# Seams between layers: x transposed before the whole last product, rounded tiles signalled one by one, half of a weight split moved behind the second rows

## The chip, the cores and the metric

The kernel runs on one core of a Trainium2 chip. TensorE (PE in the profile) multiplies and transposes, ScalarE (ACT) and VectorE (DVE) work on what it leaves in PSUM and on the weights, GpSimd (POOL) does small statistics and some loads, SyncE (SP) issues the loads of the weights. The metric is the time of one execution on the device in microseconds; of each kernel several executions are timed and the median is given. One further execution was taken with the hardware profiler, and all rows of the trace come from it.

## The reference

Two blocks of two layers each are applied to x, 256 rows of 1024 numbers. Each layer normalizes x, applies a mixer (attention with a state-space branch, a gated linear recurrence, and two kinds of attention with a memory) and adds the result; then it normalizes again, applies a gated feed-forward network and adds that result.

```python
# first block: the result is normalized before it is added
hn = rms_norm(x, norm_mix_pre[layer])
mix = even_mixer(hn, ...)  or  odd_mixer(hn, ...)
x = x + rms_norm(mix, norm_mix_post[layer])
hn = rms_norm(x, norm_ffn_pre[layer])
x = x + rms_norm(swiglu(hn, w_gate, w_up, w_down), norm_ffn_post[layer])

# second block: the result is added as it is
h = _rmsnorm(x, norm_mix[i])
x = x + jnp.concatenate([mix, mem_out], axis=-1) @ w_out[i]
x = x + _swiglu(_rmsnorm(x, norm_ffn[i]), w_gate_up[i], w_down[i])
```

So x is updated eight times, and seven of these updates are followed at once by a product of the new x with the next weights. These seven places are the seams. They are numbered 1 to 7 here, as `ed` is in the code (`ed` 0 is the first use of x, `ed` 8 the last update). At seams 1 to 4 the result is normalized before it is added, at seams 5 to 7 it is added as it is.

## The kernel before

**Products.** Every float32 product is made as three products of rounded values: each operand is held as a rounded high part and a rest (`WH` and `WL` for the weights, `HTh` and `HTl` for the transposed x, `YAh` and `YAl` for other inputs), and high by high, high by rest and rest by high are added in PSUM. Lines 452 to 454 are these three in most places; lines 487, 488 and 490 are the same three in `edge_product`, which is used for the first product after a seam.

**Weights.** They come in 200 chunks of 128 x 2048 numbers, in the order of use, through three buffers each of `RAW`, `WH` and `WL`. ACT rounds a chunk into `WH` (line 1076; line 1086 where it does a first half alone), DVE subtracts to get `WL` (line 1694; line 1702 for a first half alone). The loop `feed(c)` of an engine splits every chunk up to number c + 3 that it hasn't split yet. DVE signals a finished chunk through the semaphore `lo`, and the chunk with number c is finished when `lo` has reached c + 4. A first half alone gives no signal: `lo` goes up after the second half.

**A seam.** x has two row tiles of 128 rows (t = 0 and 1). The last two chunks before a seam are multiplied first for t = 0, then for t = 1, so that x of t = 0 can be updated while TensorE works on t = 1. In `wide_mm` this runs as follows. DVE updates x for t = 0 (lines 1736 and 1743 at seams 1 to 4, line 1730 at seams 5 to 7). PE transposes it in eight pieces (`turn`, line 458) into the PSUM banks 4 and 5, and multiplies on. ACT copies the eight pieces as rounded tiles into `HTh` with the gain of the norm (line 1093), DVE makes the rests `HTl` (line 1711). Each piece is one k, a tile of 128 of the 1024 numbers of a row. Then PE starts `edge_mm` of the next layer: for t = 0 and k = 0 to 7 three matmuls each, then the same for t = 1. The weights for k = 0 to 3 are the first chunk of the next layer, those for k = 4 to 7 the second one, and before k = 0 and before k = 4 PE waits until `lo` says that the whole chunk is there:

```python
if t == 0 and k % per == 0:
    e.wait_ge(S.lo, c + 4)
```

The second chunk of the next layer is the one that `feed(cs[-2], ed)` splits in two halves at the seam, since cs[-2] + 3 is its number. DVE updates x for t = 1 last; PE transposes that in two groups of four inside `edge_mm`, after the k given by `WHEN` (k = 5 at seams 1 to 4, k = 3 at seams 5 to 7) and after the k behind it.

**Order.** Each engine has its own program, written out by hand; an engine takes its instructions in that order, and waits are on semaphores alone. No scheduler moves anything.

Of the kernel before, what the change touches and what calls it, by code (L numbers as in the profile page):

```python
# [7 lines left out]
CH = 2048  # L8
NR = 3
NW = 3  # L10
# [236 lines left out]
def program(nc, A, PLAN, NCH):  # L247
    f32, f32r, i32 = mybir.dt.float32, mybir.dt.float32r, mybir.dt.int32
    ALU, ACT, AX = mybir.AluOpType, mybir.ActivationFunctionType, mybir.AxisListType
    MUL, ADD, SUB = ALU.mult, ALU.add, ALU.subtract  # L250
# [7 lines left out]
    with top:  # L258
        S = Signals(*[top.enter_context(nc.semaphore("s_" + n)) for n in SIGNALS.split()])
        scope = [top]  # L260

        def sb(name, shape, dt=f32):
            return scope[-1].enter_context(nc.sbuf_tensor(name, shape, dt))

        X = sb("X", [128, 2, 1024])
        HTh, HTl = sb("HTh", [128, 8, 256], f32r), sb("HTl", [128, 8, 256], f32r)
# [8 lines left out]
        RAW = sb("RAW", [128, NR, CH])  # L275
        WH, WL = sb("WH", [128, NW, CH], f32r), sb("WL", [128, NW, CH], f32r)
# [7 lines left out]
        PS = top.enter_context(nc.psum_tensor("PS", [128, 8, 512], f32))  # L284

        def col(name, i=0, n=1):
            return cst[:, COL[name] + i:COL[name] + i + n]
# [130 lines left out]
        def x_n(ed, t, half):  # L418
            return 4 * (ed - 1) + 2 * t + half + 1

        def turn_n(ed, t, j):
            return 4 * ed + 2 * t + j + 1

        def htlo_n(ed, t, k):
            return 16 * ed + 8 * t + k + 1
# [24 lines left out]
        def pe(e):  # L450
# [5 lines left out]
            def transp(out, src):  # L456
                p = src.shape[0]
                return e.transpose(out, src, ident[0:p, 0:p])  # L458
# [15 lines left out]
            def turn(ed, t, halves=(0, 1)):  # L474
                for j in halves:
                    if ed:
                        e.wait_ge(S.x, x_n(ed, t, j))
                    for i in range(4):
                        k = 4 * j + i
                        tk = transp(PS[:, 4 + 2 * t + j, 128 * i:128 * i + 128], X[:, t, 128 * k:128 * k + 128])  # L480
                    tk.then_inc(S.turn, 1)

            def edge_product(ed, c, out, t, k, w):
                ts = slice(128 * t, 128 * t + 128)
                if k % 4 == 0:
                    e.wait_ge(S.hthi, turn_n(ed, t, k // 4))
                e.matmul(out, HTh[:, k, ts], WH[:, c % NW, w], start=k == 0, stop=False)  # L487
                e.matmul(out, HTh[:, k, ts], WL[:, c % NW, w], start=False, stop=False)  # L488
                e.wait_ge(S.htlo, htlo_n(ed, t, k))
                return e.matmul(out, HTl[:, k, ts], WH[:, c % NW, w], start=False, stop=k == 7)  # L490
# [52 lines left out]
                    if hook:  # L543
                        hook(ci)

            def wide_mm(cs, ed, src_of, before, behind=None, free0=None):
                n = len(cs)

                def next_turn():
                    if free0:  # L550
                        free0()
                    turn(ed, 0)

                def both(c, k, t, between=None):
                    hi, lo, j = src_of(k)
                    for half in range(2):
                        if half and between:
                            between()
                        o = (k % 2) * 1024 + half * 512
                        tk = product(c, PS[:, 2 * t + half, :], (hi, lo), j, t, slice(o, o + 512), k == 0, k == 2 * n - 1)  # L560
                    return tk

                for ci, c in enumerate(cs[:-2]):
                    e.wait_ge(S.lo, c + 4)
                    before(ci)
                    for t in range(2):
                        for k in (2 * ci, 2 * ci + 1):
                            tk = both(c, k, t)
                    tk.then_inc(S.used, 1)
                    if ci == 0 and behind:  # L570
                        behind()
                for t in range(2):
                    for i in range(4):
                        c = cs[n - 2 + i // 2]
                        if t == 0 and i % 2 == 0:
                            e.wait_ge(S.lo, c + 4)
                            before(n - 2 + i // 2)
                        tk = both(c, 2 * n - 4 + i, t, next_turn if t == 1 and i == 3 and ed < 8 else None)
                        if t == 0 and i == 3:
                            tk.then_inc(S.half, 1)  # L580
                        if t == 1 and i % 2:
                            tk.then_inc(S.used, 1)
# [489 lines left out]
        def act(e):  # L1072
            n_split = [1]
# [18 lines left out]
            def copy(out, src, scale=1.0):  # L1092
                return e.activation(out, src, ACT.Copy, scale=scale)  # L1093
# [4 lines left out]
            def turn(ed, t, then=None):  # L1098
                name, gi = GAINS[ed]
                ts = slice(128 * t, 128 * t + 128)  # L1100
                for j in range(2):
                    e.wait_ge(S.turn, turn_n(ed, t, j))
                    for i in range(4):
                        k = 4 * j + i
                        tk = copy(HTh[:, k, ts], PS[:, 4 + 2 * t + j, 128 * i:128 * i + 128], col(name, gi + k))
                    tk.then_inc(S.hthi, 1)
                    if then:
                        then(j)

# [579 lines left out]
        def dve(e):  # L1689
            n_split = [1]  # L1690
            dv = Tally()

            def split_lo(c, w=slice(0, CH)):
                e.tensor_tensor(WL[:, c % NW, w], RAW[:, c % NR, w], WH[:, c % NW, w].bitcast(f32), SUB).then_inc(S.lo, 1)  # L1694

            def feed(c, ed=0):

                while n_split[0] <= min(c + NW, NCH - 1):
                    n = n_split[0]
                    if ed:  # L1700
                        e.wait_ge(S.hi2, ed)
                        e.tensor_tensor(WL[:, n % NW, 0:1024], RAW[:, n % NR, 0:1024], WH[:, n % NW, 0:1024].bitcast(f32), SUB)
                    e.wait_ge(S.hi, n + 4)
                    split_lo(n, slice(1024, CH) if ed else slice(0, CH))
                    n_split[0] = n + 1

            def rest(out, src, hi, gain=None):
# [8 lines left out]
            def turn(ed, t, then=None):  # L1716
                name, gi = GAINS[ed]
                ts = slice(128 * t, 128 * t + 128)
                for j in range(2):
                    e.wait_ge(S.hthi, turn_n(ed, t, j))  # L1720
                    for i in range(4):
                        k = 4 * j + i
                        rest(HTl[:, k, ts], PS[:, 4 + 2 * t + j, 128 * i:128 * i + 128], HTh[:, k, ts], col(name, gi + k)).then_inc(S.htlo, 1)
                    if then:
                        then(j)

            def add(ed, t):
                for hf in range(2):
                    x = X[:, t, 512 * hf:512 * hf + 512]
                    e.tensor_tensor(x, PS[:, 2 * t + hf, :], x, ADD).then_inc(S.x, 1)  # L1730
# [7 lines left out]
            def post_add(ed, t):  # L1738
                e.wait_ge(S.rs, RSTD[f"p{ed}{t}"])
                for hf in range(2):  # L1740
                    x = X[:, t, 512 * hf:512 * hf + 512]
                    e.wait_ge(S.yg, 4 * (ed - 1) + 2 * t + hf + 1)
                    e.scalar_tensor_tensor(x, YG[:, t, 512 * hf:512 * hf + 512], st[:, t:t + 1], x, MUL, ADD).then_inc(S.x, 1)
# [12 lines left out]
            def wide_mm(cs, ed, behind=None, after=()):  # L1756
                for ci, c in enumerate(cs[:-2]):
                    if ci == 0 and behind:
                        behind()
                    feed(c)  # L1760
                    if ci < len(after):
                        after[ci]()
                if ed <= 4:
                    e.wait_ge(S.c_bc, 16 * ed)
                    post_gain(ed, 0)
                    post_add(ed, 0)
                    feed(cs[-2], ed)
                    turn(ed, 0, lambda j: post_gain(ed, 1) if j == 0 else None)
                    post_add(ed, 1)
                    return  # L1770
                e.wait_ge(S.half, ed)
                add(ed, 0)
                if ed < 8:
                    feed(cs[-2], ed)
                    turn(ed, 0)
                e.wait_ge(S.used, cs[-1] + 1)
                add(ed, 1)

            def ffn(f, ed, beside=None):
                cs = PLAN[FFNS[f]]  # L1780
# [782 lines left out]
        @block.vector  # L2563
        def _(e):
            dve(e)
# [32 lines left out]
```

## Time and profile before

| | |
|---|---|
| time, median of 3 (lowest, highest) | 1268.29 us (1267.94, 1268.82) |
| profiled execution, its own time | 1269.22 us |
| its span, first to last instruction | 1267.4 us |
| PE busy | 1243.8 us, 98% of the span |
| DVE busy | 811.5 us, 64% |
| ACT busy | 671.7 us, 53% |
| DMA, mean over the span | 171 GB/s |

The profile counts an engine as busy from an instruction's start to its end; matmuls overlap, so their rate is read from the distance of their starts and not from their durations. A row of the timeline has the start, the time from the first start to the last end of the instructions merged in it, the engine, the line, the operation with out<-in, the count, and in brackets how long the engine was idle before it and what it waited for. In the code after the change the lines move a little: the first matmul of `edge_product` is then line 486, the split line 1687.

### The profile page before, as it was taken

What the parts mean: (1) busy time and instruction counts of PE and PEld (TensorE: products, weight loads), DVE (VectorE), ACT (ScalarE), POOL (GpSimd) and SP (SyncE); (2) the same over time, 40 slices, a digit from 0 to 9 for tenths busy, and PEclk for the clock granted to TensorE, in tenths of its full rate; (3) what the DMA queues carried; (4) which work ended last, traced back from release to release, by engine and by line L of the source; (5) the groups of instructions that cost most, each with busy time, mean ns of one, the idle gap of its engine ahead of it and who ended that gap; (6) DMA issues with size and microseconds to landing.
All of it is one profiled execution on the core that took longest, in us unless ns stands there. A gap on an engine that the chain in (4) does not pass through costs nothing.

```text
span 1267.4 us, 15790 instructions
## 1 busy us (share of the span) xinstructions
PE 1243.8 (98%) x6366; PEld 1030.2 (81%) x6366; DVE 811.5 (64%) x1034; ACT 671.7 (53%) x981; POOL 90.1 (7%) x121
## 2 busy tenths in 40 slices
PE   7999999999999999999999999999999999999998
PEld 6778888888887888888888888888888888888886
DVE  7995766644787766553687756556547774656542
ACT  7765654433897644443687535444436654544431
POOL 2410000000110100000133100000001200000000
PEclk9999999999999999999999999999999999999999
DMA  7334555555554565555554224555555324555541
GB/s 299 102 122 157 186 194 175 196 170 195 185 197 168 169 216 195 182 184 191 180 200 167 67 101 166 199 190 176 187 184 179 126 101 137 195 187 179 198 169 64
DMA packets 32392, 216.60 MB, mean 171 GB/s; under 512 B 3888, under 2 KB 4272, under 8 KB 7232
## 3 DMA queue, kind: packets, MB, share of 16 engines
q1 hardware_dynamic: 30240, 210.19, 47.9%
q0 software_dynamic: 1360, 4.78, 1.2%
q8 instruction: 50, 0.82, 0.3%
q10 hardware_dynamic: 720, 0.63, 0.1%
q14 instruction: 22, 0.18, 0.0%
HBM read 214.54 MB, written 1.05 MB: 170 GB/s over the span
## 4 chain that ended last, share of the span: by engine, by line
PE 83%; DVE 9%; ACT 4%; issue 3%; POOL 1%; DMA 0%; DVEq 0%; SPq 0%; ACTq 0%
PE PS L452 23%; PE PS L454 23%; PE PS L453 23%; PE PS L458 5%; PE PS L487 2%; PE PS L490 2%; PE PS L488 2%; DVE WL L1694 2%; PE PS L737 2%; ACT WH L1076 1%; PE PS L761 1%; ACT HTh L1093 1%; DVE YG L1971 1%; DVE YG L1961 0%; DVE st L1831 0%
## 5 line engine op out<-in xcount | busy, mean ns | idle before, releaser
L1694 DVE TENSOR_TENSOR WL<-RAW,WH 128x2048 fp32r<-128x2048 f32 (+2 forms) x200 | 443.3, 2219 | 322.3 <-ACT WH L1076 322.2
L1076 ACT ACTIVATE WH<-RAW 128x2048 fp32r<-128x2048 f32 (+2 forms) x200 | 370.8, 1857 | 373.8 <-PE PS L454 373.8
L452 PE MATMUL PS<-WH,HTh 128*128 128x512 f32 (+1 forms) x848 | 334.7, 395 | 0.0
L454 PE MATMUL PS<-WH,HTl 128*128 128x512 f32 (+1 forms) x848 | 329.0, 388 | 0.0
L453 PE MATMUL PS<-WL,HTh 128*128 128x512 f32 (+1 forms) x848 | 328.3, 387 | 0.0
L454 PEld LDWEIGHTS PS<-WH,HTl 128*128 128x128 f32 x848 | 159.2, 188 | 33.3
L452 PEld LDWEIGHTS PS<-WH,HTh 128*128 128x128 f32 x848 | 159.3, 188 | 31.9 <-DVE WL L1694 1.0
L453 PEld LDWEIGHTS PS<-WL,HTh 128*128 128x128 f32 x848 | 159.5, 188 | 30.6
L452 PE MATMUL PS<-WH,YAh 128*128 128x512 f32 x402 | 158.9, 395 | 1.6 <-DVE YAl L1710 1.2
L454 PE MATMUL PS<-WH,YAl 128*128 128x512 f32 x402 | 156.8, 390 | 0.0
L453 PE MATMUL PS<-WL,YAh 128*128 128x512 f32 x402 | 156.5, 389 | 0.0
L452 PEld LDWEIGHTS PS<-WH,YAh 128*128 128x128 f32 x402 | 75.5, 188 | 17.7 <-issue 3.0
L454 PEld LDWEIGHTS PS<-WH,YAl 128*128 128x128 f32 x402 | 75.4, 188 | 16.0
L453 PEld LDWEIGHTS PS<-WL,YAh 128*128 128x128 f32 x402 | 75.6, 188 | 14.9
L2384 POOL TENSOR_SCALAR st<-st 128x2 f32<-128x2 f32 (+4 forms) x33 | 19.3, 584 | 769.7 <-ACT JK L1112 699.0
L487 PE MATMUL PS<-WH,HTh 128*128 128x512 f32 (+1 forms) x128 | 52.6, 411 | 3.5 <-DVE WL L1694 2.1
L1093 ACT ACTIVATE HTh<-PS,cst 128x128 fp32r<-128x128 f32 (+1 forms) x136 | 39.2, 379 | 26.9 <-PE PS L458 26.9
L490 PE MATMUL PS<-WH,HTl 128*128 128x512 f32 (+1 forms) x128 | 50.3, 393 | 0.0
L488 PE MATMUL PS<-WL,HTh 128*128 128x512 f32 (+1 forms) x128 | 50.3, 393 | 0.0
L1711 DVE SCALAR_TENSOR_TENSOR HTl<-PS,cst,HTh 128x128 fp32r<-128x128 f32 (+1 forms) x136 | 39.0, 351 | 14.3 <-ACT HTh L1093 13.7
L2386 POOL TENSOR_TENSOR st<-st,mh 128x2 f32<-128x2 f32 (+4 forms) x33 | 39.7, 1202 | 2.7
L1093 ACT ACTIVATE YAh<-PS 128x512 fp32r<-128x512 f32 x38 | 21.6, 584 | 29.1 <-PE PS L458 29.1
(362 smaller groups left out, 1484.0 us busy)
## 6 DMA issues: line engine op xcount, KB each, us to landing
RAW<-in_w SPq DMA_DIRECT2D x196, 1024.0 KB, 4.9
BC<-in_rows POOLq DMA_DIRECT2D x4, 512.0 KB, 4.0
YG<-in_mem POOLq DMA_DIRECT2D x4, 512.0 KB, 4.9
X<-in_x SPq DMA_DIRECT2D x2, 512.0 KB, 5.5
RAW<-in_w SPq DMA_DIRECT2D x4, 256.0 KB, 5.7
BC<-in_s SPq DMA_DIRECT2D x1, 512.0 KB, 11.5
YG<-in_s SPq DMA_DIRECT2D x1, 512.0 KB, 11.7
BB<-in_s SPq DMA_DIRECT2D x1, 512.0 KB, 12.5
```

Source lines behind the costliest of these rows:

```text
L452: e.matmul(out, ah, bh, start=start, stop=False)
L453: e.matmul(out, ah, bl, start=False, stop=False)
L454: return e.matmul(out, al, bh, start=False, stop=stop)
L458: return e.transpose(out, src, ident[0:p, 0:p])
L487: e.matmul(out, HTh[:, k, ts], WH[:, c % NW, w], start=k == 0, stop=False)
L488: e.matmul(out, HTh[:, k, ts], WL[:, c % NW, w], start=False, stop=False)
L490: return e.matmul(out, HTl[:, k, ts], WH[:, c % NW, w], start=False, stop=k == 7)
L1076: e.activation(WH[:, c % NW, w], RAW[:, c % NR, w], ACT.Copy).then_inc(S.hi, 1)
L1093: return e.activation(out, src, ACT.Copy, scale=scale)
L1694: e.tensor_tensor(WL[:, c % NW, w], RAW[:, c % NR, w], WH[:, c % NW, w].bitcast(f32), SUB).then_inc(S.lo, 1)
L1711: return e.scalar_tensor_tensor(out, src, gain, hi.bitcast(f32), MUL, SUB)
L2386: e.tensor_tensor(st[:, at:at + n], st[:, at:at + n], mh[:, 0:n], ALU.pow).then_inc(S.rs, 1)
```

## The change

It makes three edits, at all seams alike.

1. `wide_mm` of PE: the transposes of the new x (t = 0) stood between the first and the second half of the last product (each half is three matmuls of 512 columns); now they stand ahead of both halves.
2. `turn` of ACT signals `hthi` after every rounded tile and not after the fourth. `edge_product` of PE waits before every k for that tile alone, where it waited for four tiles at k = 0 and k = 4. DVE's `turn` still waits for all four tiles.
3. `wide_mm` of DVE: the split of the next layer's second chunk stood as two halves ahead of the rests `HTl`. The first half stays there, the second half now comes after the rests and after the update of x for t = 1.

```diff
             def edge_product(ed, c, out, t, k, w):
                 ts = slice(128 * t, 128 * t + 128)
-                if k % 4 == 0:
-                    e.wait_ge(S.hthi, turn_n(ed, t, k // 4))
+                e.wait_ge(S.hthi, htlo_n(ed, t, k))
                 e.matmul(out, HTh[:, k, ts], WH[:, c % NW, w], start=k == 0, stop=False)
                 e.matmul(out, HTh[:, k, ts], WL[:, c % NW, w], start=False, stop=False)
                 e.wait_ge(S.htlo, htlo_n(ed, t, k))
...
-                        tk = both(c, 2 * n - 4 + i, t, next_turn if t == 1 and i == 3 and ed < 8 else None)
+                        if t == 1 and i == 3 and ed < 8:
+                            turn(ed, 0)
+                        tk = both(c, 2 * n - 4 + i, t)
...
                     for i in range(4):
                         k = 4 * j + i
-                        tk = copy(HTh[:, k, ts], PS[:, 4 + 2 * t + j, 128 * i:128 * i + 128], col(name, gi + k))
-                    tk.then_inc(S.hthi, 1)
+                        copy(HTh[:, k, ts], PS[:, 4 + 2 * t + j, 128 * i:128 * i + 128], col(name, gi + k)).then_inc(S.hthi, 1)
...
+            def feed_half(ed, h):
+                n = n_split[0]
+                if h == 0:
+                    e.wait_ge(S.hi2, ed)
+                    e.tensor_tensor(WL[:, n % NW, 0:1024], RAW[:, n % NR, 0:1024], WH[:, n % NW, 0:1024].bitcast(f32), SUB)
+                else:
+                    e.wait_ge(S.hi, n + 4)
+                    split_lo(n, slice(1024, CH))
                     n_split[0] = n + 1
...
                 for j in range(2):
-                    e.wait_ge(S.hthi, turn_n(ed, t, j))
+                    e.wait_ge(S.hthi, htlo_n(ed, t, 4 * j + 3))
...
                     post_gain(ed, 0)
                     post_add(ed, 0)
-                    feed(cs[-2], ed)
+                    feed_half(ed, 0)
                     turn(ed, 0, lambda j: post_gain(ed, 1) if j == 0 else None)
                     post_add(ed, 1)
+                    feed_half(ed, 1)
                     return
                 e.wait_ge(S.half, ed)
                 add(ed, 0)
                 if ed < 8:
-                    feed(cs[-2], ed)
+                    feed_half(ed, 0)
                     turn(ed, 0)
                 e.wait_ge(S.used, cs[-1] + 1)
                 add(ed, 1)
+                if ed < 8:
+                    feed_half(ed, 1)
```

The order of the instructions shows this at seam 1. On DVE before, from the update of x for t = 0 (the first row) to the update for t = 1 (the last two); `YG` holds the result times the gain of the norm behind it:

```order
L1743 SCALAR_TENSOR_TENSOR X<-YG,st,X 128x512 [waits s_yg]
L1702 TENSOR_TENSOR WL<-RAW,WH 128x1024 [waits s_hi2]
L1694 TENSOR_TENSOR WL<-RAW,WH 128x1024 [waits s_hi]
L1711 SCALAR_TENSOR_TENSOR HTl<-PS,cst,HTh 128x128 [waits s_hthi]
L1711 SCALAR_TENSOR_TENSOR HTl<-PS,cst,HTh 128x128 x3
L1736 TENSOR_TENSOR YG<-PS,BC 128x512 [waits s_sq]
L1736 TENSOR_TENSOR YG<-PS,BC 128x512
L1711 SCALAR_TENSOR_TENSOR HTl<-PS,cst,HTh 128x128 [waits s_hthi]
L1711 SCALAR_TENSOR_TENSOR HTl<-PS,cst,HTh 128x128 x3
L1743 SCALAR_TENSOR_TENSOR X<-YG,st,X 128x512 [waits s_yg,s_rs]
L1743 SCALAR_TENSOR_TENSOR X<-YG,st,X 128x512 [waits s_yg]
```

And in the changed kernel on the same engine at the same place (a first half is line 1701, a second half line 1687 there):

```order
L1743 SCALAR_TENSOR_TENSOR X<-YG,st,X 128x512 [waits s_yg]
L1701 TENSOR_TENSOR WL<-RAW,WH 128x1024 [waits s_hi2]
L1711 SCALAR_TENSOR_TENSOR HTl<-PS,cst,HTh 128x128 [waits s_hthi]
L1711 SCALAR_TENSOR_TENSOR HTl<-PS,cst,HTh 128x128 x3
L1736 TENSOR_TENSOR YG<-PS,BC 128x512 [waits s_sq]
L1736 TENSOR_TENSOR YG<-PS,BC 128x512
L1711 SCALAR_TENSOR_TENSOR HTl<-PS,cst,HTh 128x128 [waits s_hthi]
L1711 SCALAR_TENSOR_TENSOR HTl<-PS,cst,HTh 128x128 x3
L1743 SCALAR_TENSOR_TENSOR X<-YG,st,X 128x512 [waits s_yg,s_rs]
L1743 SCALAR_TENSOR_TENSOR X<-YG,st,X 128x512 [waits s_yg]
L1687 TENSOR_TENSOR WL<-RAW,WH 128x1024 [waits s_hi]
```

The second half of the split moved from the third place to the last, past eight rests and four instructions of the update of x.

On PE before, at the end of the last product of seam 1, from its first half to the first matmul of the next layer:

```order
L452 MATMUL PS<-WH,YAh 128x512
L453 MATMUL PS<-WL,YAh 128x512
L454 MATMUL PS<-WH,YAl 128x512
L458 MATMUL PS<-ident,X 128x128 [waits s_x]
L458 MATMUL PS<-ident,X 128x128 x3
L458 MATMUL PS<-ident,X 128x128 [waits s_x]
L458 MATMUL PS<-ident,X 128x128 x3
L452 MATMUL PS<-WH,YAh 128x512
L453 MATMUL PS<-WL,YAh 128x512
L454 MATMUL PS<-WH,YAl 128x512
L487 MATMUL PS<-WH,HTh 128x512 [waits s_hthi,s_lo]
```

And in the changed kernel:

```order
L458 MATMUL PS<-ident,X 128x128 [waits s_x]
L458 MATMUL PS<-ident,X 128x128 x3
L458 MATMUL PS<-ident,X 128x128 [waits s_x]
L458 MATMUL PS<-ident,X 128x128 x3
L452 MATMUL PS<-WH,YAh 128x512
L453 MATMUL PS<-WL,YAh 128x512
L454 MATMUL PS<-WH,YAl 128x512
L452 MATMUL PS<-WH,YAh 128x512
L453 MATMUL PS<-WL,YAh 128x512
L454 MATMUL PS<-WH,YAl 128x512
L486 MATMUL PS<-WH,HTh 128x512 [waits s_hthi,s_lo]
```

The eight transposes moved three matmuls forward; nothing else moved there.

The third place is on PE in the next layer, k = 3 and k = 4 of t = 0. Before:

```order
L487 MATMUL PS<-WH,HTh 128x512
L488 MATMUL PS<-WL,HTh 128x512
L490 MATMUL PS<-WH,HTl 128x512 [waits s_htlo]
L487 MATMUL PS<-WH,HTh 128x512 [waits s_hthi,s_lo]
L488 MATMUL PS<-WL,HTh 128x512
L490 MATMUL PS<-WH,HTl 128x512 [waits s_htlo]
```

And in the changed kernel:

```order
L486 MATMUL PS<-WH,HTh 128x512 [waits s_hthi]
L487 MATMUL PS<-WL,HTh 128x512
L489 MATMUL PS<-WH,HTl 128x512 [waits s_htlo]
L486 MATMUL PS<-WH,HTh 128x512 [waits s_hthi,s_lo]
L487 MATMUL PS<-WL,HTh 128x512
L489 MATMUL PS<-WH,HTl 128x512 [waits s_htlo]
```

No instruction moved here; k = 3 has a wait for its own rounded tile, and k = 4 keeps its wait for the second chunk (`s_lo`).

## Rows read from the trace of the kernel before

**Rows 1.** Page, part 1: busy us, share of the span, instructions.

```profile
PE 1243.8 (98%) x6366; PEld 1030.2 (81%) x6366; DVE 811.5 (64%) x1034; ACT 671.7 (53%) x981; POOL 90.1 (7%) x121
```

**Rows 2.** Page, part 4: the chain that ended last, by engine.

```profile
PE 83%; DVE 9%; ACT 4%; issue 3%; POOL 1%; DMA 0%; DVEq 0%; SPq 0%; ACTq 0%
```

**Rows 3.** Line 487, its idle time by releaser: us, times.

```profile
  DVE WL L1694: 8.8, 9
  ACT HTh L1093: 1.3, 7
```

**Rows 4.** Timeline of PE at seam 1 (columns as told above).

```profile
130.03 0.40 PE L454 MATMUL PS<-WH,YAl 128*128 128x512 f32 x1
130.62 0.47 PE L487 MATMUL PS<-WH,HTh 128*128 128x512 f32 x1 [0.19 <-ACT HTh L1093]
...
131.16 0.40 PE L490 MATMUL PS<-WH,HTl 128*128 128x512 f32 x1
...
133.22 0.39 PE L490 MATMUL PS<-WH,HTl 128*128 128x512 f32 x1
133.45 0.39 PE L487 MATMUL PS<-WH,HTh 128*128 128x512 f32 x1
```

**Rows 5.** Timeline of DVE at seam 1.

```profile
128.01 1.23 DVE L1702 TENSOR_TENSOR WL<-RAW,WH 128x1024 fp32r<-128x1024 f32 x1
129.15 1.22 DVE L1694 TENSOR_TENSOR WL<-RAW,WH 128x1024 fp32r<-128x1024 f32 x1
130.51 1.13 DVE L1711 SCALAR_TENSOR_TENSOR HTl<-PS,cst,HTh 128x128 fp32r<-128x128 f32 x4
131.62 1.29 DVE L1736 TENSOR_TENSOR YG<-PS,BC 128x512 f32<-128x512 f32 x2
132.82 1.12 DVE L1711 SCALAR_TENSOR_TENSOR HTl<-PS,cst,HTh 128x128 fp32r<-128x128 f32 x4
133.86 1.40 DVE L1743 SCALAR_TENSOR_TENSOR X<-YG,st,X 128x512 f32<-128x512 f32 x2
```

**Rows 6.** Timeline of ACT at seam 1.

```profile
127.88 1.04 ACT L1076 ACTIVATE WH<-RAW 128x1024 fp32r<-128x1024 f32 x1
129.34 1.14 ACT L1093 ACTIVATE HTh<-PS,cst 128x128 fp32r<-128x128 f32 x4 [0.41 <-PE PS L458]
130.47 1.02 ACT L1112 ACTIVATE JK<-PS 128x1024 f32<-128x1024 f32 x1
```

**Rows 7.** Timeline of PE at seam 4, where the update of x is late.

```profile
620.34 0.36 PE L487 MATMUL PS<-WH,HTh 128*128 128x448 f32 x1
...
621.35 0.37 PE L490 MATMUL PS<-WH,HTl 128*128 128x448 f32 x1
621.86 0.66 PE L458 MATMUL PS<-ident,X 128*128 128x128 f32 x4
```

**Rows 8.** Timeline of DVE at seam 4, update of x for t = 1.

```profile
621.06 1.40 DVE L1743 SCALAR_TENSOR_TENSOR X<-YG,st,X 128x512 f32<-128x512 f32 x2
```

**Rows 9.** Timeline of all engines at seam 5.

```profile
770.74 1.05 ACT L1076 ACTIVATE WH<-RAW 128x1024 fp32r<-128x1024 f32 x1
...
772.20 2.17 ACT L1093 ACTIVATE HTh<-PS,cst 128x128 fp32r<-128x128 f32 x8 [0.41 <-PE PS L458]
...
775.45 1.28 DVE L1730 TENSOR_TENSOR X<-PS,X 128x512 f32<-128x512 f32 x2
...
776.67 0.48 PE L487 MATMUL PS<-WH,HTh 128*128 128x512 f32 x1
```

**Rows 10.** Page, part 2: granted TensorE clock, tenths, in 40 slices.

```profile
PEclk9999999999999999999999999999999999999999
```

**Rows 11.** Timeline of PE at the start of the kernel.

```profile
9.31 0.79 PE L487 MATMUL PS<-WH,HTh 128*128 128x512 f32 x1 [2.13 <-DVE WL L1694]
...
14.60 0.45 PE L488 MATMUL PS<-WL,HTh 128*128 128x512 f32 x1
```

**Rows 12.** Timeline of PE after a wait of 1.16 us inside a layer.

```profile
405.13 0.47 PE L452 MATMUL PS<-WH,YAh 128*128 128x512 f32 x1 [1.16 <-DVE YAl L1710]
```

More of the change, by code:

```diff
@@ L544, in rows_mm, with wide_mm, both @@
                         hook(ci)
-            def wide_mm(cs, ed, src_of, before, behind=None, free0=None):
+            def wide_mm(cs, ed, src_of, before, behind=None):
                 n = len(cs)
[L549 to L554, printed above, removed]
+                def both(c, k, t):
                     hi, lo, j = src_of(k)
                     for half in range(2):
-                        if half and between:
-                            between()
                         o = (k % 2) * 1024 + half * 512
@@ L1694, in split_lo, with feed @@
                 e.tensor_tensor(WL[:, c % NW, w], RAW[:, c % NR, w], WH[:, c % NW, w].bitcast(f32), SUB).then_inc(S.lo, 1)
-            def feed(c, ed=0):
+            def feed(c):
                 while n_split[0] <= min(c + NW, NCH - 1):
                     n = n_split[0]
-                    if ed:
-                        e.wait_ge(S.hi2, ed)
-                        e.tensor_tensor(WL[:, n % NW, 0:1024], RAW[:, n % NR, 0:1024], WH[:, n % NW, 0:1024].bitcast(f32), SUB)
                     e.wait_ge(S.hi, n + 4)
-                    split_lo(n, slice(1024, CH) if ed else slice(0, CH))
+                    split_lo(n)
+                    n_split[0] = n + 1
+            def feed_half(ed, h):
[6 more added lines that the diff above has]
+                    split_lo(n, slice(1024, CH))
                     n_split[0] = n + 1
```

## The prediction, made before the changed kernel ran

> **What bounds the kernel now.** I read the page's shares first. PE is busy for 1243.8 of 1267.4 us, DVE for 64% and ACT for 53% [rows 1]; the reader is to see that PE leaves only some 24 us, so that nearly every microsecond in which PE stands still is a microsecond of the result. The chain of waits says the same in another way: 83% of it is PE, and the 9% of DVE and 4% of ACT are the short pieces in which PE's next instruction hung on them [rows 2]. No load is on it (DMA 0%). So the question for each edit is only what PE waits for at the seven seams, before and after.
>
> Next I asked for the idle time of the first matmul behind a seam, line 487. It sat idle for `WL` 8.8 us in 9 cases and for `HTh` 1.3 us in 7 [rows 3]. This answer can mislead: the split that ends just before each seam is that of the second chunk, while k = 0 needs the first one. The names are given by the semaphore that moved last. So I went to the timelines of seam 1, which show it in full.
>
> PE: the last old matmul starts at 130.03, the first new one at 130.62, 0.59 later, where the distance inside a run of matmuls is 0.23 (133.22 to 133.45). The restart then costs a little more: from 130.62 to the third matmul at 131.16 it takes 0.54, not 0.46 [rows 4]. So a seam loses 0.36 + 0.08 = 0.44 us before. ACT begins the rounded tiles at 129.34 after 0.41 idle, and four of them end at 130.48 [rows 6]; DVE's second half split ends at 129.15 + 1.22 = 130.37, and the rests start at 130.51 [rows 5]. Both are late by the same amount, which is why the three edits come together. PE reaches k = 4 at 133.45, for which the second chunk had been finished since 130.37.
>
> **Edit 1, transposes before the whole last product.** They move three matmuls forward, 3 x 0.23 = 0.69 us. The number of instructions and of changes between kinds stays. x is there: DVE's update of t = 0 is over before 128.01 [rows 5], and PE would begin the transposes at about 128.0, the second four of them at 128.4. ACT can use only part of the 0.69: its own split ends at 127.88 + 1.04 = 128.92 [rows 6], so the tiles start there and not at 129.34. That is 0.42 us earlier; four tiles are there at 130.06.
>
> **Edit 2, tiles signalled one by one.** PE's k = 0 then needs only the first tile, at about 129.2, but its third matmul needs the first rest, and DVE still waits for four tiles: 130.06 plus one rest (four take 1.13, so about 0.3) is 130.4. PE would like that third matmul at 130.26 + 0.46 = 130.72. It is met. More signals on ACT and more waits on PE are not shown for these forms; the nearest row is DVE, which signals every rest and makes four in 1.13, against 1.14 for ACT's four with one signal [rows 5, 6]. From both sides: nothing, or at most 0.1 us a tile on ACT, 0.4 for the four tiles before k = 0, which would use up the gain of edit 1. I take nothing.
>
> **Edit 3, the late half.** With 1 and 2, taking 1.14 us (129.15 - 128.01) of DVE from ahead of the rests lets them start when the tiles are there. All three together close the seam: PE starts the next layer at 130.03 + 0.23 = 130.26. The gain is 0.36 + 0.08 = 0.44 us a seam, at most 3.1 us over seven.
>
> But k = 4 keeps its wait for the whole second chunk, and the signal comes only behind the late half. At seam 1 DVE goes on, in the new order: four rests, the gain (131.62), four rests (132.82), the update of x for t = 1 (133.86 to 135.26) [rows 5]. None of this gets earlier by the edit: the gain at 131.62 waits for ACT's squares, which start at 130.47 when PE has finished the old product [rows 6], and PE finishes that when it did before. The rows overlap by 0.08 (132.82 + 1.12 against 133.86), so the late half runs from 135.18 to 135.18 + 1.22 = 136.40 [rows 5]. PE can start k = 4 about 0.1 us behind it; that distance is the one at seam 4, where x is half done at 621.06 + 0.70 = 621.76 and PE's transposes start at 621.86 [rows 7, 8]. So k = 4 starts at 136.5 instead of 133.45: 3.03 us late, and with 0.08 for the restart 3.1 us. PE would have been ready at 133.0; it stands still for 3.5 us, and the 0.44 us that were gained are used up in it. Behind the waiting instruction on PE is everything: k = 5 to 7, the transposes of x for t = 1, and through these ACT and DVE.
>
> Seams 2 and 3 have the same rows at other times, to 0.02 us. Seam 4 has matmuls of 448 columns: the late half ends at 621.06 + 1.40 - 0.08 + 1.22 = 623.60, k = 4 starts at 623.70 instead of 620.34, 3.36 + 0.08 late [rows 7, 8]. There PE waited before for x ahead of the transposes, 621.35 to 621.86, 0.51 where 0.20 would do; that 0.3 goes, x being long there. So 3.1 again. Four such seams: 12.4 us.
>
> Seams 5 to 7 have a shorter chain on DVE: eight rests and the plain update. At seam 5 ACT's split ends at 770.74 + 1.05 = 771.79, so the tiles start there and not at 772.20; rests and update follow 0.41 to 0.5 us earlier (I take 0.45), and the update ends at 775.45 + 1.28 - 0.45 = 776.28. The late half ends at 776.28 - 0.08 + 1.22 = 777.42, k = 4 starts at 777.5 instead of 776.67 [rows 9]. That is 0.8 us late. The restart is no extra, since k = 4 came behind transposes before as well. Seams 6 and 7 are alike: 3 x 0.8 = 2.4 us.
>
> **Sum.** 12.4 + 2.4 = 14.8 us slower. Against the profiled execution, 1269.2, that is 1284.0; it lies 0.9 us above the median of the runs, 1268.3, so the predicted median is 1283.1. Downstream I count nothing back: PE is the bound, and what it does later starts later by the same.
>
> Bounds: PE's start behind the late half, 0 to 0.2 us a seam, makes -0.7 to +0.7 over seven. Signals on ACT, up to 0.1 us a tile, are hidden at seams 1 to 4 in ACT's wait for PE (tiles end at 130.06, squares start at 130.47), and add up to 0.8 us on each of seams 5 to 7 through the eight rests; the eight tiles of t = 1 could add as much at all seven where their cover fails. I put +4 for the two as the upper end.
>
> **Rivals.**
> *A, the clock falls in the stall.* The first matmuls of the kernel, after idle stretches, run slow: from 9.31 to 14.60 there are ten matmuls of 512 columns and four transposes, 5.3 us where 0.23 each, 0.4 and two restarts make 2.9 [rows 11]; the granted clock of the page reads 9 tenths or more even in that slice [rows 10], so only the durations tell. If a stall of over 3 us puts PE back to the lower of its two levels (1.2 instead of 2.4 GHz), each of seams 1 to 4 costs 2.4 us more, 9.6 in all: 1292.7. Against it: behind a wait of 1.16 us the first matmul lasted 0.47 [rows 12], as the first one of a seam does [rows 4], and not 0.79 as at the start [rows 11]; seams 5 to 7 wait about as long. No wait of 3 us lies in this trace behind the start. The Trainium skill (TensorE: Matmul & The Clock Gate, section on HAM oscillation) tells of a kernel in which the array waited a few microseconds between bursts and each burst began at half the clock; by that page this rival would be the rule, and no row here shows whether it holds for one stall alone. Chance 0.08.
>
> *B, other side: the late half is hidden, and the kernel is faster.* It needs the signal for the second chunk by 133.0 at seam 1, when PE is due at k = 4. For it: before, the chunk was finished 3.1 us ahead of its use (130.37 against 133.45), so there is slack to spend. Against it: the late half ends at 136.4, 3.4 us past that, and its chain is tied to PE's own last matmul. It could only be so if k = 4 waited for another chunk than the moved one; cs[-2] + 3 is the second chunk of the next layer, so I don't see how. It would give 7 x 0.44 = 3.1 us: 1265.2. Chance 0.03.
>
> *C, part of the loss is given back.* PE's idle time inside the layers, as the 1.16 us of [rows 12], could shrink where DVE or ACT catch up during the stall. For it: PE has some 24 us of idle time in all [rows 1]. Against it: 5 to 9 of these lie at the start, about 3 at the seams, and the waits inside layers hang on products that move with PE. Perhaps 4 us come back: 1279.1. Chance 0.07.
>
> **How the numbers follow.** The forecast holds with 0.82. Its own range is 1281.5 to 1287: the bounds above, and 1 us for how runs of the same kernel lie (1267.9 to 1268.8). The range for 8 in 10 takes in rival C at the lower end, 1279, and 1288 above; A and B stay out. What a measurement of this kernel can tell from no change is about 0.2%, 2.5 us. Rival B alone is on the faster side, and at 3.1 us it just passes that bound: faster 0.02, same 0.02, slower 0.96.
>
> **What would show it.** At seam 1 of the changed kernel the first matmul of the next layer should start 0.23 us behind the last old one, with no idle time for `HTh`. Then k = 0 to 3 in 2.7 us, and at k = 4 an idle time of PE of 3.1 to 3.3 us (from the modelled end of the matmul before), put down to `WL` of line 1687; four of these and three of about 1.0 us. DVE's late half should stand behind the update of x for t = 1 and PE start within 0.1 us of its end. ACT's tiles should still take 1.14 for four; 1.5 would show a price of the signals. Durations of 0.63 behind the stall would show rival A. I am wrong if k = 4 starts without idle time, or if DVE reaches the late half much earlier than I say, which would mean that the squares on ACT do not wait for the end of the old product.

## The result, and the profile after

| | before | changed |
|---|---|---|
| median, 5 runs each | 1268.32 us | 1291.43 us |
| lowest, highest | 1267.94, 1268.82 | 1289.26, 1292.00 |
| ratio, 95% interval | 1 | 1.0178 (1.0167 to 1.0189) |
| span of the profiled execution | 1267.4 us | 1289.6 us |

The changed kernel is 23.1 us slower by the medians; the spans differ by 22.2 us, because the profiled execution of the kernel before (1269.22 us) lay 0.9 us above its median while that of the changed kernel is its median. That is on the forecast side, but past the forecast of 1283.1 and past its range, which ended at 1288. The page of the changed kernel shows PE busy longer with the same number of matmuls, DVE with more of the chain, and a row that was all nines before [rows 10] has one eight:

```profile
PE 1251.6 (97%) x6366; PEld 1036.6 (80%) x6366; DVE 811.9 (63%) x1034; ACT 671.2 (52%) x981; POOL 90.8 (7%) x121
...
PEclk9999999999899999999999999999999999999999
...
PE 81%; DVE 11%; ACT 5%; issue 2%; POOL 1%; DMA 0%; DVEq 0%; SPq 0%; ACTq 0%
```

Busy time of PE rose by 7.8 us against [rows 1]; a longer wait alone would not do that. The idle time of line 486, which was line 487 in [rows 3], names the wait. Taken together with the weight loads of that line, as [rows 3] are, it is 39.2 us in 16 cases; for the matmuls alone it is:

```profile
  DVE WL L1687: 18.2, 8
```

Of these 2.1 us are one wait at the start, which the kernel before has too [rows 11]; the other seven are one at each seam, 16.1 us together.

Seam 1 on PE answers to [rows 4]. The first new matmul starts 0.23 us behind the last old one (130.22, 130.45), without idle time. Then k = 4 waits 3.28 us:

```profile
130.22 0.39 PE L454 MATMUL PS<-WH,YAl 128*128 128x512 f32 x1
130.45 0.40 PE L486 MATMUL PS<-WH,HTh 128*128 128x512 f32 x1
...
130.91 0.40 PE L489 MATMUL PS<-WH,HTl 128*128 128x512 f32 x1
...
132.96 0.39 PE L489 MATMUL PS<-WH,HTl 128*128 128x512 f32 x1
136.63 0.50 PE L486 MATMUL PS<-WH,HTh 128*128 128x512 f32 x1 [3.28 <-DVE WL L1687]
```

And on DVE, which answers to [rows 5], the late half is the last row; it ends at 136.57, and PE starts 0.06 behind it. The first row is ACT's, with the four rounded tiles:

```profile
129.00 1.12 ACT L1087 ACTIVATE HTh<-PS,cst 128x128 fp32r<-128x128 f32 x4
...
130.15 1.13 DVE L1711 SCALAR_TENSOR_TENSOR HTl<-PS,cst,HTh 128x128 fp32r<-128x128 f32 x4 [0.75 <-ACT HTh L1087]
131.79 1.29 DVE L1736 TENSOR_TENSOR YG<-PS,BC 128x512 f32<-128x512 f32 x2 [0.52 <-ACT JK L1105]
133.00 1.12 DVE L1711 SCALAR_TENSOR_TENSOR HTl<-PS,cst,HTh 128x128 fp32r<-128x128 f32 x4
134.03 1.41 DVE L1743 SCALAR_TENSOR_TENSOR X<-YG,st,X 128x512 f32<-128x512 f32 x2
135.35 1.22 DVE L1687 TENSOR_TENSOR WL<-RAW,WH 128x1024 fp32r<-128x1024 f32 x1
```

What the forecast did not count is seen best at seam 2, behind the standstill:

```profile
330.10 0.80 PE L486 MATMUL PS<-WH,HTh 128*128 128x512 f32 x1 [3.27 <-DVE WL L1687]
330.69 0.63 PE L487 MATMUL PS<-WL,HTh 128*128 128x512 f32 x1
331.12 0.63 PE L489 MATMUL PS<-WH,HTl 128*128 128x512 f32 x1
...
335.67 0.67 PE L486 MATMUL PS<-WH,HTh 128*128 128x512 f32 x1
336.18 0.40 PE L487 MATMUL PS<-WL,HTh 128*128 128x512 f32 x1
```

Until 336.18 the matmuls behind the first start 0.43 us apart and not 0.23, as they do at the start of the kernel [rows 11]. The granted clock of the stretches says it too. The columns are the stretch, its length, busy us (and instructions) of PE, PEld, DVE, ACT and POOL, the granted clock, and share and GB/s of the loads:

```profile
128.00:134.00 6.00, 5.35 (x28) 4.17 (x26) 4.69 (x12) 4.26 (x12) 0.80 (x2) 1.00 0.01 5
134.00:142.00 8.00, 5.37 (x20) 4.48 (x21) 3.70 (x8) 1.79 (x7) 0.62 (x1) 0.79 0.54 197
...
327.00:337.00 10.00, 6.90 (x22) 5.64 (x23) 4.20 (x11) 2.09 (x8) 1.67 (x3) 0.66 0.64 239
```

```profile
795.89 0.60 PE L458 MATMUL PS<-ident,X 128*128 128x128 f32 x4
797.39 0.50 PE L486 MATMUL PS<-WH,HTh 128*128 128x512 f32 x1 [0.90 <-DVE WL L1687]
797.72 0.39 PE L487 MATMUL PS<-WL,HTh 128*128 128x512 f32 x1
```

The length of each seam in the timeline of PE, from the start of the last old matmul to the start of the first one behind the 48 of `edge_product`, shows where the whole difference is. All kernels of this study stand in it, each by its one profiled execution:

| us | seam 1 | 2 | 3 | 4 | 5 | 6 | 7 | sum against before |
|---|---|---|---|---|---|---|---|---|
| before | 12.50 | 12.50 | 12.50 | 11.68 | 12.50 | 12.48 | 12.49 | |
| changed | 17.26 | 18.43 | 16.93 | 16.41 | 13.22 | 13.18 | 13.24 | +22.0 |
| only_late | 17.21 | 17.25 | 17.00 | 16.35 | 13.79 | 13.78 | 13.79 | +22.5 |
| fill | 15.64 | 15.64 | 15.65 | 14.75 | 13.22 | 13.18 | 13.23 | +14.7 |
| fill_few | 17.27 | 15.62 | 15.61 | 16.38 | 13.24 | 13.17 | 13.24 | +17.9 |
| halves | 13.81 | 13.82 | 13.82 | 13.09 | 12.06 | 12.06 | 12.05 | +4.1 |
| no_late | 12.39 | 12.38 | 12.40 | 11.67 | 12.17 | 12.12 | 12.17 | -1.4 |
| only_turn | 12.39 | 12.39 | 12.40 | 11.69 | 12.18 | 12.12 | 12.19 | -1.3 |
| only_tiles | 12.39 | 12.37 | 12.40 | 11.68 | 12.42 | 12.42 | 12.43 | -0.5 |
| gains | 12.48 | 12.47 | 12.49 | 11.87 | 12.17 | 12.16 | 12.18 | -0.8 |

The spans differ by 22.2 us, the seams by 22.0: what was lost or given back elsewhere comes to 0.2 us.

### The profile page after: what moved, and what is told of

It is laid out like the page before. It is cut to its first block, busy times and chain, and to the rows that moved or that the text cites. A ratio compares the mean times of both kernels' runs of the same rounds, so it can differ in the third digit from the quotient of the medians.

```text
span 1289.6 us, 15794 instructions
## 1 busy us (share of the span) xinstructions
PE 1251.6 (97%) x6366; PEld 1036.6 (80%) x6366; DVE 811.9 (63%) x1034; ACT 671.2 (52%) x981; POOL 90.8 (7%) x121
## 3 DMA queue, kind: packets, MB, share of 16 engines
HBM read 214.54 MB, written 1.05 MB: 167 GB/s over the span
## 4 chain that ended last, share of the span: by engine, by line
PE 81%; DVE 11%; ACT 5%; issue 2%; POOL 1%; DMA 0%; DVEq 0%; SPq 0%; ACTq 0%
PE PS L452 22%; PE PS L454 22%; PE PS L453 22%; PE PS L458 5%; DVE WL L1687 3%; PE PS L486 2%; PE PS L489 2%; PE PS L487 2%; PE PS L731 2%; ACT WH L1070 2%; PE PS L755 1%; DVE HTl L1711 1%; DVE YG L1974 1%; ACT JK L1105 1%; DVE YG L1964 0%
## 5 line engine op out<-in xcount | busy, mean ns | idle before, releaser
L452 PEld LDWEIGHTS PS<-WH,HTh 128*128 128x128 f32 x848 | 159.3, 188 | 31.9 <-DVE WL L1687 0.9
L453 PEld LDWEIGHTS PS<-WL,YAh 128*128 128x128 f32 x402 | 75.6, 188 | 14.8
L486 PEld LDWEIGHTS PS<-WH,HTh 128*128 128x128 f32 x128 | 26.0, 203 | 25.3 <-DVE WL L1687 21.0
## 6 DMA issues: line engine op xcount, KB each, us to landing
BB<-in_s SPq DMA_DIRECT2D x1, 512.0 KB, 12.5
```

The source lines that it names most:

```text
L452: e.matmul(out, ah, bh, start=start, stop=False)
L453: e.matmul(out, ah, bl, start=False, stop=False)
```

## The experiments

My theory after the result: the late half holds k = 4 as forecast, and in the long standstill TensorE's clock falls. The rivals: the slow matmuls come from the added signals and waits of edit 2, or from work beside them; or something else than the wait for the second chunk holds PE.

**only_late**, edit 3 alone on the kernel before (the diff is that of `feed_half` and of the seam on DVE, as shown in the section on the change):

```diff
-                    feed(cs[-2], ed)
+                    feed_half(ed, 0)
                     turn(ed, 0, lambda j: post_gain(ed, 1) if j == 0 else None)
                     post_add(ed, 1)
+                    feed_half(ed, 1)
```

> The kernel before with edit 3 alone: the second half split behind the update of x for t = 1; transposes and signals as before. My theory (the late half holds k = 4, and in the long standstill TensorE's clock falls): the late half ends at 136.4 us at seam 1 as in the changed kernel, so k = 4 is late by 3.1 us at seams 1 to 4 and by 1.3 us at seams 5 to 7, 16 us in all, and PE stands still a little shorter than in the changed kernel, 2.9 instead of 3.3 us. With the slow stretches of the changed kernel (1.4 to 2.9 us at each of seams 1 to 4) 1290 to 1294; if 2.9 us is too short for the clock to fall, 1284.5. The rival, that the slow matmuls come from the signals and waits of edit 2, says 1284.5 with durations of 0.39 throughout.

Measured: 1289.81 us against 1268.96 for the kernel before in the same job, ratio 1.0167 (1.0154 to 1.0181), just under the 1290 to 1294 that I expected. PE stands still for 2.82 us, and is slow behind it without any edit of the signals:

```profile
132.29 0.39 PE L490 MATMUL PS<-WH,HTl 128*128 128x512 f32 x1
135.50 0.56 PE L487 MATMUL PS<-WH,HTh 128*128 128x512 f32 x1 [2.82 <-DVE WL L1694]
135.85 0.63 PE L488 MATMUL PS<-WL,HTh 128*128 128x512 f32 x1
```

So edit 3 makes nearly the whole loss by itself, clock and all, and the rival of edit 2's signals falls.

How often the clock falls differs between executions of one kernel. The four of only_late took 1290.73, 1288.90, 1288.27 and 1293.10 us at a mean granted clock of 0.995, 0.997, 0.997 and 0.992; the first is the profiled one, in which the clock fell at all four long standstills. 0.997 is also what the profiled execution of fill_few has, in which it fell at two. So in the table above a row of a kernel with long standstills is one draw, and the medians of the times carry more.

**no_late**, edits 1 and 2 without edit 3:

```diff
                     feed_half(ed, 0)
+                    feed_half(ed, 1)
                     turn(ed, 0, lambda j: post_gain(ed, 1) if j == 0 else None)
                     post_add(ed, 1)
-                    feed_half(ed, 1)
...  (the same at seams 5 to 7)
```

> The changed kernel with edit 3 undone: both half splits stand ahead of the rests again, transposes early and tiles signalled one by one. My theory: no standstill at k = 4 and no slow matmul; PE gains 0.3 to 0.44 us at each of seven seams, its first rest comes a little late because DVE ends the split at 130.4: 1265.3 to 1266.2. The rival, that the signals and waits of edit 2 cost time, says 1268.5 or more, with the tiles of a group of four taking over 1.3 us.

Measured: 1267.67 us against 1268.96 for the kernel before in the same job, ratio 0.9991 (0.9982 to 1.0000). No standstill at k = 4 and no slow matmul, but less gained than expected. The timeline of PE at seam 1 shows both ends:

```profile
130.33 0.39 PE L454 MATMUL PS<-WH,YAl 128*128 128x512 f32 x1
130.56 0.40 PE L486 MATMUL PS<-WH,HTh 128*128 128x512 f32 x1
...
134.53 0.39 PE L489 MATMUL PS<-WH,HTl 128*128 128x512 f32 x1
134.95 0.66 PE L458 MATMUL PS<-ident,X 128*128 128x128 f32 x4
135.36 0.47 PE L486 MATMUL PS<-WH,HTh 128*128 128x512 f32 x1
```

And DVE, the update of x for t = 1:

```profile
134.15 1.41 DVE L1743 SCALAR_TENSOR_TENSOR X<-YG,st,X 128x512 f32<-128x512 f32 x2
```

The first new matmul follows at once, which wins 0.35 us up to k = 4. But the transposes of x for t = 1 come 0.42 us behind the matmul before them, where it was 0.23. PE is early and x is not, since its update hangs on the end of the old product: the update starts 3.82 us behind the last old matmul (130.33 to 134.15), where it was 3.83 (130.03 in [rows 4] to 133.86 in [rows 5]). Of 0.35 us some 0.11 are left at seams 1 to 3. At seam 4, where the transposes waited for x before as well [rows 7], 0.01 is left, and at seams 5 to 7 it is 0.34.

**fill**, the changed kernel with idle work for PE where it would stand still:

```diff
+                        if t == 0 and k == 4:
+                            for _ in range(14 if ed < 5 else 4):
+                                e.matmul(PS[:, banks[1], :], HTh[:, 0, 0:128], WH[:, cs[0] % NW, 0:512], start=True, stop=True)
                         if t == 0 and k % per == 0:
                             e.wait_ge(S.lo, c + 4)
```

> The changed kernel with idle work for PE: before k = 4 of t = 0 it runs 14 more matmuls of 512 columns at seams 1 to 4 and 4 at seams 5 to 7, into the PSUM bank that t = 1 overwrites, so that it isn't idle while the late half is made. The results don't change. My theory (the clock falls because PE stands still): k = 4 starts at the same distance from the last old matmul, 6.4 us at seam 1, but the matmuls behind it keep their distance of 0.23: the 7.6 us of slow stretches go, 1283.5 to 1284.5. The rival, that the slow stretches come from edit 2 or from DVE's and ACT's work beside PE, says 1291 as before.

Measured: 1282.79 us, ratio 1.0109 (1.0095 to 1.0123), 0.7 us under what I expected. k = 4 starts as late as in the changed kernel, 6.41 us behind the last old matmul (129.67 to 136.08), and runs on at full speed:

```profile
132.41 0.39 PE L489 MATMUL PS<-WH,HTl 128*128 128x512 f32 x1
132.64 3.33 PE L517 MATMUL PS<-WH,HTh 128*128 128x512 f32 x14
136.08 0.50 PE L486 MATMUL PS<-WH,HTh 128*128 128x512 f32 x1
136.42 0.40 PE L487 MATMUL PS<-WL,HTh 128*128 128x512 f32 x1
```

The granted clock of the same stretch as above is back at 1.00:

```profile
134.00:142.00 8.00, 7.89 (x39) 6.24 (x38) 4.28 (x11) 3.76 (x9) 0.62 (x1) 1.00 0.57 197
```

This settles the size. The wait costs 14.7 us in the seams, and the clock 1.6, 2.8, 1.3 and 1.7 at seams 1 to 4 (changed less fill in the table), 7.4 us. PE works more here than in the changed kernel, and the median is 8.6 us lower (1282.79 against 1291.43, from two jobs; the ratios to the kernel before in each job, 1.0109 and 1.0178, say the same).

**halves**, the changed kernel with a signal for the first half alone:

```diff
-                        if t == 0 and k % per == 0:
+                        if t == 0 and k == 0 or t == 0 and k == 6:
                             e.wait_ge(S.lo, c + 4)
+                        if t == 0 and k == 4:
+                            e.wait_ge(S.loh, ed)
...  (on DVE, the first half split)
-                    e.tensor_tensor(WL[:, n % NW, 0:1024], RAW[:, n % NR, 0:1024], WH[:, n % NW, 0:1024].bitcast(f32), SUB)
+                    e.tensor_tensor(WL[:, n % NW, 0:1024], RAW[:, n % NR, 0:1024], WH[:, n % NW, 0:1024].bitcast(f32), SUB).then_inc(S.loh, 1)
```

> The changed kernel, but the first half split has a signal of its own, and k = 4 waits for that alone; the whole second chunk is waited for at k = 6, where its second half is used. My theory: at seams 1 to 4 k = 4 and 5 run at once, k = 6 waits for the late half and starts 1.5 us later than in the kernel before; at seams 5 to 7 the late half is there in time and 0.4 us are gained: 4 x 1.5 - 3 x 0.4 = 4.8, 1273. If PE's clock falls after a standstill of 1.5 us too, up to 8 us more. The rival, that something else than the wait on the second chunk holds PE, says a standstill at k = 4 as in the changed kernel, 1291.

Measured: 1272.57 us, ratio 1.0027 (1.0016 to 1.0037). The standstill moved to k = 6 and shrank to 1.14 us, and the clock held:

```profile
134.50 0.66 PE L458 MATMUL PS<-ident,X 128*128 128x128 f32 x4
136.30 0.50 PE L486 MATMUL PS<-WH,HTh 128*128 128x512 f32 x1 [1.14 <-DVE WL L1689]
136.63 0.40 PE L487 MATMUL PS<-WL,HTh 128*128 128x512 f32 x1
```

So it was the wait for the second chunk, and no other, that held PE. At seams 5 to 7 the late half is in time for k = 6 and 0.42 to 0.44 us a seam are won: the largest gain there of all kernels. At seams 1 to 4 the late half still costs 1.3 to 1.4 us.

**only_turn**, edit 1 alone:

```diff
-                        tk = both(c, 2 * n - 4 + i, t, next_turn if t == 1 and i == 3 and ed < 8 else None)
+                        if t == 1 and i == 3 and ed < 8:
+                            turn(ed, 0)
+                        tk = both(c, 2 * n - 4 + i, t)
```

> The kernel before with edit 1 alone: transposes ahead of both halves of the last product. ACT's tiles start 0.4 us earlier, so the fourth is there at about 130.06 at seam 1, before PE wants k = 0 at 130.26; DVE's first rest comes at 130.85, 0.1 after PE wants it. My theory: the gain of a seam is there once, not once per edit, so this alone makes what edits 1 and 2 make together: the first new matmul 0.23 us behind the last old one, a seam of 12.39 us at seams 1 to 4 and 12.15 at seams 5 to 7 where it was 12.50, 1.3 us in all. The rival, that the terms of edits 1 and 2 add, says half of that or less: 0.3 to 0.7 us.

Measured: 1267.44 us against 1268.63, ratio 0.9990 (0.9981 to 0.9999). In the seams it is no_late to 0.02 us, so edit 2 adds nothing to edit 1: the two close the same gap. Its median is the lowest of the study, though not told from that of no_late; these two are the only ones whose interval does not reach past the kernel before.

**only_tiles**, edit 2 alone: no_late with the transposes put back between the two halves.

```diff
                     for half in range(2):
+                        if half and between:
+                            between()
...
-                        if t == 1 and i == 3 and ed < 8:
-                            turn(ed, 0)
-                        tk = both(c, 2 * n - 4 + i, t)
+                        tk = both(c, 2 * n - 4 + i, t, (lambda: turn(ed, 0)) if t == 1 and i == 3 and ed < 8 else None)
```

> The kernel before with edit 2 alone: tiles signalled and waited for one by one, transposes in their old place. The first tile is there at 129.7, so the first new matmul follows the last old one by 0.23 us too; the fourth tile ends at 130.48, DVE's first rest at 130.86, 0.14 after PE wants it. My theory: the same 1.0 to 1.3 us as with both edits, for the same reason. The rival, that the gain is edit 1's: nothing, 0 to 0.2 us.

Measured: 1268.30 us, ratio 0.9997 (0.9988 to 1.0005), not told from no change. I had expected 1.0 to 1.3 us. The seams of the table give 0.5: what I expected held at seams 1 to 3 and not at 5 to 7. The first new matmul starts at once with edit 2 alone too, but the rests still come as late as before, and the third matmul waits (at seam 1):

```profile
130.26 0.39 PE L487 MATMUL PS<-WL,HTh 128*128 128x512 f32 x1
130.67 0.50 PE L489 MATMUL PS<-WH,HTl 128*128 128x512 f32 x1
```

It starts 0.41 us behind the second, where the others have 0.23. At seams 5 to 7 DVE's chain runs from the rests straight to the update of x, so late rests mean late transposes. Edit 1, which starts the tiles earlier, won 0.30 to 0.36 us a seam there (only_turn), edit 2 alone 0.06 to 0.08.

**gains**, no_late with the update of x for t = 1 made half by half at seams 1 to 4:

```diff
-                    turn(ed, 0, lambda j: post_gain(ed, 1) if j == 0 else None)
-                    post_add(ed, 1)
+                    turn(ed, 0, lambda j: post_gain(ed, 1, (0,)) if j == 0 else None)
+                    post_add(ed, 1, (0,))
+                    post_gain(ed, 1, (1,))
+                    post_add(ed, 1, (1,))
...  (post_gain and post_add take the halves that they are to do)
```

> Edits 1 and 2 without edit 3, and one change more: at seams 1 to 4 DVE updates x of t = 1 half by half. It makes the gain of the first half, the four rests, the update of the first half, then gain and update of the second half. With edits 1 and 2 alone PE gained 0.35 us by k = 4 of seam 1 and lost 0.25 of it again 1.5 us later, at the transposes of x for t = 1, which wait for that update (idle from 134.53 + 0.23 to 134.95). My theory: the first half of x is ready 0.6 us earlier, the wait goes, and seams 1 to 4 take 12.15 us or less instead of 12.39: 1266.5 to 1267.0 where edits 1 and 2 alone gave 1267.7, both against 1269.0 for the kernel before. The rival, that the 0.25 is lost to something else (the rests, ACT's tiles): no difference from edits 1 and 2 alone.

Measured: 1268.09 us, ratio 0.9996 (0.9987 to 1.0004). A miss:

```profile
133.07 0.39 PE L489 MATMUL PS<-WH,HTl 128*128 128x512 f32 x1
133.35 0.66 PE L458 MATMUL PS<-ident,X 128*128 128x128 f32 x4
...
134.30 0.40 PE L489 MATMUL PS<-WH,HTl 128*128 128x512 f32 x1
134.74 0.66 PE L458 MATMUL PS<-ident,X 128*128 128x128 f32 x4
```

The first four transposes are nearly in time now, 0.28 behind the matmul before them and not 0.42, but the second four come 0.44 behind theirs: the second half of x is later than before. It is done 5.78 us behind the last old matmul, where no_late has 5.23 (134.15 + 1.41 less 130.33). That PE waits for x is confirmed; that the wait would go was wrong, it changed its place, and seams 1 to 3 are 0.09 us longer than in no_late, seam 4 0.20.

**fill_few**, fill with 5 matmuls at seams 1 to 4 and none at 5 to 7:

```diff
-                            for _ in range(14 if ed < 5 else 4):
+                            for _ in range(5 if ed < 5 else 0):
```

> The changed kernel with 5 idle matmuls of 512 columns before k = 4 of t = 0 at seams 1 to 4 and none at seams 5 to 7, into the PSUM bank that t = 1 overwrites; PE then stands still for 2.1 us at these seams instead of 3.3 (with 14 of them it didn't, and the slow stretches were gone). Results don't change. If the clock falls after a standstill of 2.1 us too, 1290 as in the changed kernel; if it takes more, 1283 as with 14. The standstills of 0.9 and 1.14 us seen so far left it alone, 2.8 us did not. I expect something between, since PE's idle share is smaller: 1283 to 1287.

Measured: 1286.20 us, ratio 1.0138 (1.0122 to 1.0153). In the profiled execution the clock fell at seams 1 and 4, behind standstills of 2.15 and 2.46 us, and held at seams 2 and 3, behind 2.14 us each. Seams 1 and 2 in the stretches:

```profile
134.00:142.00 8.00, 5.86 (x23) 4.51 (x22) 3.97 (x9) 1.37 (x5) 0.62 (x1) 0.79 0.56 197
328.00:336.00 8.00, 5.86 (x30) 4.70 (x30) 4.60 (x12) 3.51 (x9) 1.67 (x3) 1.00 0.65 240
```

The same work with nearly the same standstill in it (2.15 and 2.14 us) takes 17.27 and 15.62 us. The time lies in the range of 1283 to 1287 that I expected. What decides between such cases is left open.

## Why the prediction was wrong

**The step that failed** is the sum, in the sentence that k = 4 is "3.03 us late, and with 0.08 for the restart 3.1 us" at seams 1 to 4. It took the lateness of k = 4 for the whole price of the standstill. What the work behind it costs was left at the full clock and put aside as rival A with a chance of 0.08. The runs show that A is the case: in the profiled execution the clock fell behind every one of the four long standstills, and keeping PE busy (fill) takes 8.6 us off. The ground on which I held it for unlikely was a wait of 1.16 us that changed nothing [rows 12]. That row is true, and 13 standstills of 0.84 to 1.14 us at the seams of these runs bear it out, but it says nothing on 3.3 us: the nearest row was a factor of three away, and the start of the kernel [rows 11] was the only row on the other side. The clock term belonged into the sum's bounds, with both ends kept. The price of A, 2.4 us a seam, was near but high: 1.6, 2.8, 1.3 and 1.7 were measured, and 1292.7 for the whole was 1.3 us above the measured median.

**What held.** The wait was named with its place, its releaser and its size. k = 4 starts 6.41 us behind the last old matmul where [rows 4] have 3.42, 2.99 late against 3.03 forecast. PE starts 0.06 us behind the late half against 0.1. Edit 3 makes the wait alone (only_late), and the kernel with the clock held (fill) measures 1282.79, 13.8 us above the kernel before in its own job, where the sum said 14.8. In the table fill costs 12.5 us at seams 1 to 4 (12.4 in the sum) and 2.2 at seams 5 to 7 (2.4 in the sum). In the changed kernel seams 5 to 7 cost 0.70 to 0.75 us each, 0.8 forecast. Rivals B and C are out: no seam is faster, and outside the seams the spans differ by 0.2 us.

**What was right in kind and wrong in size: the gain of edits 1 and 2.** "All three together close the seam" is so: 0.23 us between old and new matmul. But the 0.44 us a seam, 3.1 in all, that I used for rival B was over twice what was left of it. Without edit 3 the seams give back 1.4 us, since at seams 1 to 4 the next wait, for x of t = 1, stands 1.5 us behind and takes most of it. I had seen that this update hangs on PE's own last matmul, used it for the late half, and not for the transposes that hang on the same chain. The terms of edits 1 and 2 do not add either: each puts the first tile ahead of PE's need.

**Two readings in the working** were off without changing the sum. The 8.8 us in 9 cases of [rows 3] I read as idle time of the first matmul behind a seam. They count matmuls and weight loads together: for the matmuls alone `WL` is named once, for 2.1 us at the start of the kernel [rows 11], and the other 6.7 us in 8 cases are weight loads. And k = 4 at 136.5 where it was at 133.45 makes 3.05 us and not 3.03.

**Costs taken as nothing** that were nothing: three more signals on ACT (four tiles take 1.12 us at seam 1 of the changed kernel, where [rows 6] have 1.14) and the added waits on PE (0.23 us a matmul as before). No memory load came into it.

## What to carry to other kernels

Work that is moved off the path of one wait can land in front of another, as here; before moving it, write down who waits for its signal and when that one is due, down the whole chain of the engine that now comes first. On an engine that sets the time, a standstill is not worth its own length alone: where it is as long as here, price the work behind it at the lower clock as well, or give the engine something harmless to do. And a gain at the head of a chain is only worth what the next wait down the same chain leaves of it.

## What the runs showed of the hardware

After standstills of 0.84 to 1.14 us between matmuls (13 cases in the changed kernel, only_late, halves and fill_few) the clock held. After 2.14 to 2.46 us (fill_few) it fell in 2 cases of 4, and after 2.82 to 3.59 us in 8 of 8 (changed kernel and only_late). These are the profiled executions alone: two others of only_late had a granted clock of 0.997 where the profiled one had 0.995, which makes, as an estimate, about half as much time at the lower clock. Behind the start of a kernel no standstill between 1.3 and 2.1 us lies in these traces. Where it fell, matmuls of 512 columns start 0.43 us apart and not 0.23, in some cases at once (330.10 at seam 2), in some 1.5 us later (in the changed kernel seam 1 starts again at 136.63, and the transposes at 138.13 are the first that are slow, 1.05 us where before it was 0.60), for about 3 to 6 us. In the changed kernel 1.3 to 2.8 us are lost by it at a seam. Rival A had the Trainium skill behind it (TensorE: Matmul & The Clock Gate, section on HAM oscillation, on a kernel whose array waited between bursts and began them at half the clock); by that rule this trace agrees at seam 2, also for one standstill inside hundreds of microseconds of dense work, with the granted clock at 0.66 in the 10 us around it. At seam 1 the work behind the standstill began at the full clock and was slow only 1.5 us later.

The start of the kernel is another matter: its matmuls are as slow [rows 11] while the granted clock reads 1.00 there, so a granted clock at the head of a trace is not to be trusted over the durations. The record of the clock in the trace of the kernel before begins only where these slow matmuls end; ahead of it 1.00 stands for want of one.
